# Two units of an output projection moved into the attention stage that comes before it

## The chip, the core and the metric

One core of one Trainium2 chip runs one program, launched once. The metric is device time in microseconds (us). Engines are named as the profile names them: PE (TensorE matmuls; PEld its weight loads), DVE (VectorE), ACT (ScalarE), POOL (GpSimd), SP (SyncE, which here only issues DMAs).

## The reference

One layer of a streaming encoder over 1,024 prompt tokens and 8 streams of 16 new tokens, 1,152 tokens (9 tiles of 128) in all, everything in float32:

```
h = RMSNorm(x)
z = h @ w_in                      # B, C, x_in (gated short convolution), q, k, v (attention)
a = B * causal_dwconv3(C * x_in)  # 1,024 columns
o = differential attention, 8 heads of 128 columns, RMSNorm per head
x = x + concat(a, o) @ w_out      # the output projection, 2048 x 2048
x = x + HierMoE(RMSNorm(x))       # top-1 of 4 expert groups, top-2 of its 8 experts
y = RMSNorm(x)
```

## The kernel before

The kernel is a row of phases, each a block of five instruction streams with waits on semaphores. At the end of a block all engines meet, so no instruction of the next phase starts earlier on any engine. In order: norm and input projection, attention of the streams (`phase_decode`), attention of the prompt (`phase_attend`), output projection with the router's logits (`phase_mix_out`), experts, final norm. The change touches `phase_attend`, `phase_mix_out` and the class `MixWeights`.

**Precision by parts.** Each float32 operand of a large product is kept as two rounded parts, hi and lo, and a product is three matmuls: hi with hi, hi with lo, lo with hi.

**`phase_attend`.** A head has eight row tiles of 128 queries, taken in four pairs of a large and a small one, 32 pairs `n` in all. Each engine's stream is a software pipeline written out by hand over `n` from -2 to 32: scores (PE), maximum (DVE), exponential (ACT), sum ratios (POOL, two tiny instructions per tile), the mix of the two score maps (DVE, L1025, the wait for POOL's ratio before it), transposes (PE, L957), weighted sum with v (PE, L971), the copy of the result (ACT, L1124). POOL also squares the finished heads (L913) and scales them (L918) between ratios, at iterations given in tables. A finished head is turned (four PE transposes per half head) and kept as `o_hi` (ACT, L1135) and `o_lo` (DVE, L1045); heads 0 to 5 and the streams' rows go through this inside the pipeline. Heads 6 and 7 come last: after the pipeline DVE squares, sums and scales head 7 while POOL scales head 6 (L918, the last one), then PE makes the 16 transposes of `LAST_OUTS` (L1003 to L1008) into the four banks of `s_big`. PSUM is full in this phase: `s_big` four banks, `s_small` two, `t_ps` and `o_ps` one each. At the end of its stream SP issues the loads of the first two units of `w_out` (L889), and at the end of its own POOL splits them into hi and lo (L931).

**`phase_mix_out`.** The tokens are taken in two passes (five tiles, then four), the 2,048 output columns in four chunks of 512: eight rounds. A round goes over the 16 row blocks `k` of `w_out`, two at a time: such a pair is a **unit**, 64 units in all, 30 matmuls each in the first pass (2 blocks x 5 tiles x 3). The first four units of a round multiply `o` (heads 0 and 1, then 2 and 3, and so on), the last four multiply `a`. A unit's weights (512 KB) are loaded by SP into one of two `raw` buffers and split by POOL into one of two `hi`/`lo` buffers: a cast (L2186) and a subtraction (L2188). The load of unit i waits for the split of unit i-2; the split of unit i waits until PE has used unit i-2 and, of course, for its load. PE waits for a unit's split before it (L1299 to L1301 are the three matmuls). At the start of the phase ACT issues eight loads of 1,152 KB that bring all of `a` from DRAM (L1351, L1352), and SP issues, in this order, the router's weights `wr` (L1249: 2,048 runs of 144 bytes) and bias `br` (L1250: 128 runs of 144 bytes), the load of unit 2, one chunk of the norm's factors `g`, the load of unit 3, the first tile of `x`, the load of unit 4, and so on.

```
if i >= 2:
    sp.wait_ge(self.split_done, i - 1)
...
for i in range(2, ROUNDS * NQ):
    unit_used(pool, i - 2)
    weights.split(pool, i)
```

Of the kernel before, what the change touches and what calls it, by code (L numbers as in the profile page):

```python
# [29 lines left out]
P = 128  # L30
# [737 lines left out]
    sp.dma_start(v[:, s, :, :], c.io.v_all[0:PROMPT, h * VD:(h + 1) * VD].rearrange("(t p) e -> p t e", p=P)).then_inc(head_loaded[s], 16)  # L768


def phase_attend(c, o_hi, o_lo, q, k_rows, v, head_loaded, first_weights):

    nc, io, sem = c.nc, c.io, c.sem
    QT = PROMPT // P
# [13 lines left out]
    OUTS = ((HEADS, 0), (HEADS, 1), (0, 0), (0, 1), (1, 0), (1, 1), (2, 0), (2, 1), (3, 0), (3, 1), (4, 0), (4, 1), (5, 0), (5, 1))  # L788
    FIRST_OUT = 16
    LAST_OUTS = ((6, 0), (6, 1), (7, 0), (7, 1))  # L790

    def out_at(n):
        return n - FIRST_OUT if 0 <= n - FIRST_OUT < len(OUTS) else None
# [14 lines left out]
    with ExitStack() as mem:  # L808
        def sb(name, shape, dt=F32):
# [24 lines left out]
        squared, summed, guarded, mean_ready = sem("a_squared"), sem("a_summed"), sem("a_guarded"), sem("a_mean_ready")  # L834
        root_ready, rstd_ready, scaled = sem("a_root_ready"), sem("a_rstd_ready"), sem("a_scaled")
        out_turned, out_hi, out_kept = sem("a_out_turned"), sem("a_out_hi"), sem("a_out_kept")
        last_squared, last_turned, last_hi, last_scaled = (sem(f"a_{n}") for n in (
            "last_squared", "last_turned", "last_hi", "last_scaled"))

        s_ps, pr, at = (s_big, s_small), (pr_big, pr_small), (at_big, at_small)  # L840

# [33 lines left out]
            return ps.rearrange("p (a n) -> p a n", a=4) if h == HEADS else ps  # L875

        def last_bank(n):
            return s_big[:, n // 2, (n % 2) * 512:(n % 2 + 1) * 512]

        with nc.Block() as block:  # L880

            @block.sync
            def _(sp):
                sp.dma_start(so[:], io.o_new.rearrange("p (a b) -> p a b", a=HEADS)).then_inc(so_loaded, 16)
                for h in range(2, HEADS):
                    sp.wait_ge(weighed, QT * (h - 1))
                    load_head(c, sp, h, q, k_rows, v, head_loaded)
                for i in range(2):
                    first_weights.load(sp, i)  # L889

            @block.gpsimd
            def _(pool):
                pool.memset(mask_k[:], 1.0).then_inc(mask_step, 1)
                pool.memset(mask_q[:], 0.0).then_inc(mask_step, 1)
                pool.wait_ge(mask_step, 2)
                for m in range(2):
                    pool.memset(mask_q[m * DH:m * DH + 1, 0:P // 2], MASKED).then_inc(mask_step, 1)

                def ratio(kind, n):

                    col = tile(kind, n)
                    pool.wait_ge(inverted[kind], n + 1)
                    pool.tensor_tensor(factor(kind, n), factor(kind, n), l[:, col, 0:1], ALU.mult).then_inc(ratios[kind], 1)
                    pool.wait_ge(ratios[kind], n + 1)
                    pool.tensor_tensor(factor(kind, n), factor(kind, n), c.neglam[:], ALU.mult).then_inc(cf_ready[kind], 1)

                def square_head(h):
                    pool.wait_ge(o_kept, QT * (h + 1))
                    if h > 0:
                        pool.wait_ge(summed, h)  # L910
                    else:
                        pool.wait_ge(so_step, 2)
                    pool.tensor_tensor(square[:], o[:, h], o[:, h], ALU.mult).then_inc(squared, 1)  # L913

                def scale(h):
                    batch = 0 if h == HEADS else [n for n, (h0, h1) in enumerate(BATCHES) if h0 <= h < h1][0]
                    pool.wait_ge(rstd_ready, batch + 1)
                    pool.tensor_tensor(rows_of(h), rows_of(h), per_row(h), ALU.mult).then_inc(scaled, 1)  # L918

                for n in range(-2, PAIRS + 1):  # L920
                    if is_pair(n + 1):
                        ratio(BIG, n + 1)
                    if is_pair(n):
                        ratio(SMALL, n)
                    if n in SQUARES:
                        square_head(SQUARES[n])
                    if n in SCALES:
                        scale(SCALES[n])
                scale(6)
                for i in range(2):  # L930
                    first_weights.split(pool, i)  # L931

            @block.tensor
            def _(pe):
# [48 lines left out]
                for n in range(-2, PAIRS + 1):  # L983
                    if is_pair(n):
                        turn(BIG, n, 0)
                    if out_at(n) is not None:
                        h, half = OUTS[out_at(n)]
                        pe.wait_ge(scaled, SCALED[h])
                        pe.wait_ge(o_kept, 2 * n - 1)
                        turn_out(o_ps[:], h, half).then_inc(out_turned, 1)  # L990
                    if is_pair(n + 2):
                        scores(BIG, n + 2)
                    if is_pair(n):
                        turn(BIG, n, 1)
                    if is_pair(n - 1):
                        weigh(SMALL, n - 1, 0)
                    if is_pair(n + 1):
                        scores(SMALL, n + 1)
                    if is_pair(n):
                        weigh(BIG, n, 0)  # L1000
                        turn(SMALL, n, 0)
                        weigh(BIG, n, 1)
                for n, (h, half) in enumerate(LAST_OUTS):  # L1003
                    if h == HEADS - 1:
                        pe.wait_ge(last_scaled, 1)
                    else:
                        pe.wait_ge(scaled, len(SCALES) + 1)
                    turn_out(last_bank(n), h, half).then_inc(last_turned, 1)  # L1008

            @block.vector  # L1010
            def _(dve):
# [88 lines left out]
                dve.tensor_tensor(rows_of(HEADS - 1), rows_of(HEADS - 1), per_row(HEADS - 1), ALU.mult).then_inc(last_scaled, 1)  # L1100
                for n, (h, half) in enumerate(LAST_OUTS):
                    dve.wait_ge(last_hi, n + 1)
                    out_lo(last_bank(n), h, half)

            @block.scalar
            def _(act):
# [54 lines left out]
                    out_hi_of(last_bank(n), h, half).then_inc(last_hi, 1)  # L1161


def phase_mix_out(c, a_hi, a_lo, o_hi, o_lo, weights):

    nc, io, sem = c.nc, c.io, c.sem
    WC = 4 * P
    NCH = D // WC
    QK = 2
    NQ = KT // QK  # L1170
    AK = 2
    FIRST = (NT + 1) // 2
    PASSES = (tuple(range(FIRST)), tuple(range(FIRST, NT)))
    ROUNDS = 2 * NCH
    with ExitStack() as mem:
        def sb(name, shape, dt=F32):
            return mem.enter_context(nc.sbuf_tensor(name, shape, dt))

        w_hi, w_lo, w_split = weights.hi, weights.lo, weights.split_done
        x = sb("m_x", [P, FIRST, WC])  # L1180
        xg = sb("m_xg", [P, FIRST, WC])
        xgT = sb("m_xgT", [P, 2, 4, P])
# [3 lines left out]
        junk = sb("m_junk", [P, 2, WC])  # L1186
        parts = sb("m_parts", [P, NT, NCH])
        ssq = sb("m_ssq", [P, NT])
        z = mem.enter_context(nc.psum_tensor("m_z", [P, FIRST, WC], F32))
        tp = mem.enter_context(nc.psum_tensor("m_tp", [P, 2, 4, P], F32))  # L1190
        lg_ps = mem.enter_context(nc.psum_tensor("m_lg", [P, 512], F32))
        g_loaded = c.sems("m_g_loaded", 2)
        x_loaded, x1_stored, xg_stored = (c.sems(f"m_{n}", FIRST) for n in ("x_loaded", "x1_stored", "xg_stored"))
        w_used, params = sem("m_w_used"), sem("m_params")
        z_done, x1_ready, xg_ready, squared = sem("m_z_done"), sem("m_x1_ready"), sem("m_xg_ready"), sem("m_squared")
        turned, turned_kept, logits_done = sem("m_turned"), sem("m_turned_kept"), sem("m_logits_done")
        summed, root_done, rstd_done, lg_step = sem("m_summed"), sem("m_root_done"), sem("m_rstd_done"), sem("m_lg_step")
# [35 lines left out]
        with nc.Block() as block:  # L1233

            @block.sync
            def _(sp):
# [9 lines left out]
                        sp.wait_ge(squared, piece(v - 1, s) + 1)  # L1246
                    sp.dma_start(x[:, s, :], rows_of(io.x, v, s)).then_inc(x_loaded[s], 16)

                sp.dma_start(wr[:], io.w_router.rearrange("(k p) n -> p k n", p=P)).then_inc(params, 16)  # L1249
                sp.dma_start(br[:], io.b_router.to_broadcast([P, NR])).then_inc(params, 16)  # L1250
                for v in range(ROUNDS):
                    for q in range(NQ):
                        if v > 0 or q >= 2:
                            weights.load(sp, v * NQ + q)
                        if q == 2:
                            load_g(v)
                        if q >= 3 and q - 3 < len(tiles(v)):
# [1 line left out]

            @block.gpsimd  # L1260
            def _(pool):
                for i in range(2, ROUNDS * NQ):
                    unit_used(pool, i - 2)
                    weights.split(pool, i)

# [1 line left out]
            def _(pe):  # L1267
# [17 lines left out]
                    mm.then_inc(logits_done, 1)  # L1285

                for v in range(ROUNDS):
                    for k in range(KT):
                        i = v * NQ + k // QK
                        if k % QK == 0:  # L1290
                            pe.wait_ge(w_split, i + 1)
# [2 lines left out]
                        for s in slots(v):  # L1294
                            if k == 0 and v > 0:
                                pe.wait_ge(x1_ready, piece(v - 1, s) + 1)
                            hi, lo = cat(k, tiles(v)[s])
                            wh, wl = w_hi[:, i % 2, k % QK, :], w_lo[:, i % 2, k % QK, :]
                            pe.matmul(z[:, s, :], hi, wh, start=(k == 0), stop=False)  # L1299
                            pe.matmul(z[:, s, :], hi, wl, start=False, stop=False)  # L1300
                            mm = pe.matmul(z[:, s, :], lo, wh, start=False, stop=(k == KT - 1))  # L1301
                            if k == KT - 1:
                                mm.then_inc(z_done, 1)
                        if k % QK == QK - 1 and k < KT - 1:
# [857 lines left out]
class MixWeights:  # L2162
# [3 lines left out]
    def __init__(self, c, mem):  # L2166
        nc, shape = c.nc, [P, 2, self.QK, self.WC]
        self.raw = mem.enter_context(nc.sbuf_tensor("m_w_raw", shape, F32))
        self.hi, self.lo = (mem.enter_context(nc.sbuf_tensor(f"m_w_{n}", shape, F32R)) for n in ("hi", "lo"))
        self.loaded, self.hi_done, self.split_done = c.sems("m_w_loaded", 2), c.sem("m_w_hi_done"), c.sem("m_w_split")  # L2170
        self.rows = c.io.w_out.rearrange("(h k p) n -> h p k n", h=2, p=P)

    def load(self, sp, i):
# [7 lines left out]

    def split(self, pool, i):

        s = i % 2
        pool.wait_ge(self.loaded[s], 16 * (i // 2 + 1))
        pool.tensor_copy(self.hi[:, s], self.raw[:, s]).then_inc(self.hi_done, 1)  # L2186
        pool.wait_ge(self.hi_done, i + 1)
        pool.tensor_tensor(self.lo[:, s], self.raw[:, s], self.hi[:, s], ALU.subtract).then_inc(self.split_done, 1)  # L2188


def build(nc, io):
# [7 lines left out]
    with ExitStack() as stack:  # L2199
# [23 lines left out]
        with ExitStack() as mem:  # L2223
# [8 lines left out]
            phase_decode(c, first_keys, keys_loaded, q, k_rows, v, head_loaded)  # L2232
            o_hi, o_lo = cat("o_hi"), cat("o_lo")
            weights = MixWeights(c, mem)
            phase_attend(c, o_hi, o_lo, q, k_rows, v, head_loaded, weights)
            a_hi, a_lo = cat("a_hi"), cat("a_lo")
            phase_mix_out(c, a_hi, a_lo, o_hi, o_lo, weights)
        c.clear_semaphores()
        with ExitStack() as mem:
            c.group_expert = mem.enter_context(nc.sbuf_tensor("group_expert", [1, SLOT_GROUPS], I32))  # L2240
# [56 lines left out]
```

## Time and profile before

| what | value |
|---|---|
| median of 3 runs | 3646.26 us (3644.12 to 3651.1) |
| span of the profiled execution | 3649.7 us |
| PE busy | 3378.6 us, 93% |
| DVE, ACT, POOL busy | 1667.7 us (46%), 1291.5 us (35%), 839.7 us (23%) |
| mean granted TensorE clock | 0.965 of full speed |
| prompt attention | from 1394 us to 1646 us after the span's start |
| output projection | from 1646 us to some 2110 us |

The span runs from the first to the last instruction. The profiled execution has no separate time of its own beside its span; the span lies 1.4 us under the slowest of the three runs and 3.4 us over their median. Times below count from the span's start. A wait is an engine's idle time before an instruction, with what released it.

### The profile page before, as it was taken

Reading aid. Unit: us, or ns where it says so; the run is one execution under the profiler, and the core shown is the slowest. Engines: PE = TensorE matmul, PEld = TensorE weight load, DVE = VectorE, ACT = ScalarE, POOL = GpSimd, SP = SyncE. Lnnn points to the kernel's source line nnn. Section 1 sums busy time; section 2 is a strip of 40 time slices with the busy share of each in tenths; the row PEclk is TensorE's granted clock in tenths of the full one; section 3 lists DMA queues with packets and bytes.
Section 4 is the critical chain, followed back from the end, with each engine's and each line's share of the span. In section 5 each row is a group of like instructions: output and inputs, shape, how many; then the busy total and the mean of one; then the engine's idle time right before and its main releaser. Section 6 shows DMA issues by size and latency. Waiting matters only on the chain. (4 is left out here: it accounts for less than half of the span.)

```text
span 3649.7 us, 51076 instructions
## 1 busy us (share of the span) xinstructions
PE 3378.6 (93%) x18429; PEld 2959.6 (81%) x18430; DVE 1667.7 (46%) x1742; ACT 1291.5 (35%) x1581; POOL 839.7 (23%) x689
## 2 busy tenths in 40 slices
PE   7999999999999887988999959999999999999990
PEld 7999999999999865656888847878888778778770
DVE  5211112100111146871021167558888858856677
ACT  4000000000000034660011037557878757746572
POOL 2223222222222211224445531101111111101010
PEclk9999999999999989998999969999999999999995
DMA  4112111212222292116344459769999969967798
GB/s 153 59 53 66 59 53 53 76 62 74 85 79 66 85 335 75 60 40 225 122 155 143 132 180 361 263 251 343 359 366 357 373 244 371 357 242 251 270 337 355
DMA packets 340683, 692.65 MB, mean 190 GB/s; under 512 B 23034, under 2 KB 150954, under 8 KB 329983
## 3 DMA queue, kind: packets, MB, share of 16 engines
q1 hardware_dynamic: 290340, 586.79, 45.3%
q10 hardware_dynamic: 37163, 66.14, 4.9%
q0 software_dynamic: 13104, 38.69, 3.0%
q8 instruction: 50, 0.82, 0.1%
q14 instruction: 26, 0.21, 0.0%
HBM read 638.29 MB, written 97.28 MB: 202 GB/s over the span
## 5 line engine op out<-in xcount | busy, mean ns | idle before, releaser
L1876 DVE TENSOR_TENSOR e_w_lo<-expert_raw,e_w_hi 128x2048 fp32r<-128x2048 f32 x388 | 872.5, 2287 | 254.7 <-ACT e_w_hi L1788 228.4
L1788 ACT ACTIVATE e_w_hi<-expert_raw 128x2048 fp32r<-128x2048 f32 x388 | 744.5, 1919 | 301.0 <-PE e_gu L1702 252.0
L280 PE MATMUL p_z<-hT_hi,p_w_hi 128*128 128x384 f32 x2256 | 755.0, 335 | 1.6 <-DVE p_xs L399 1.6
L282 PE MATMUL p_z<-hT_hi,p_w_lo 128*128 128x384 f32 x2256 | 753.6, 334 | 0.0
L281 PE MATMUL p_z<-hT_lo,p_w_hi 128*128 128x384 f32 x2256 | 753.6, 334 | 0.0
L280 PEld LDWEIGHTS p_z<-hT_hi,p_w_hi 128*128 128x128 f32 x2256 | 423.5, 188 | 1.9 <-DVE p_xs L399 1.9
L281 PEld LDWEIGHTS p_z<-hT_lo,p_w_hi 128*128 128x128 f32 x2256 | 423.5, 188 | 0.0
L282 PEld LDWEIGHTS p_z<-hT_hi,p_w_lo 128*128 128x128 f32 x2256 | 423.4, 188 | 0.0
L1702 PE MATMUL e_gu<-e_w_hi,e_xT_hi 128*128 128x512 f32 x1216 | 390.1, 392 | 6.3 <-issue 6.2
L1702 PE MATMUL e_gu<-e_w_lo,e_xT_hi 128*128 128x512 f32 x1216 | 387.5, 390 | 0.0
L1702 PE MATMUL e_gu<-e_w_hi,e_xT_lo 128*128 128x512 f32 x1216 | 387.4, 390 | 0.0
L266 POOL CAST p_w_hi<-p_w_raw 128x1024 fp32r<-128x1024 f32 x96 | 100.4, 1046 | 895.2 <-issue 427.4
L1702 PEld LDWEIGHTS e_gu<-e_w_hi,e_xT_hi 128*128 128x128 f32 x1216 | 226.8, 188 | 60.3 <-issue 14.6
L1702 PEld LDWEIGHTS e_gu<-e_w_lo,e_xT_hi 128*128 128x128 f32 x1216 | 228.6, 188 | 48.1
L1702 PEld LDWEIGHTS e_gu<-e_w_hi,e_xT_lo 128*128 128x128 f32 x1216 | 228.6, 188 | 47.8
L736 ACT ACTIVATE d_kT<-d_t 128x512 f32<-128x512 f32 x32 | 19.1, 596 | 662.8 <-PE d_t L619 662.8
L268 POOL TENSOR_TENSOR p_w_lo<-p_w_raw,p_w_hi 128x1024 fp32r<-128x1024 f32 x96 | 235.5, 2453 | 7.7
L486 ACT ACTIVATE p_e_hi<-p_e 128x1152 fp32r<-128x1152 f32 x8 | 9.3, 1168 | 576.0 <-DVEq L438 576.0
L1679 PE MATMUL e_y_ps<-e_w_hi,e_aT_hi 128*128 128x512 f32 x608 | 198.9, 408 | 14.9 <-DVE e_w_lo L1876 6.9
L1542 POOL COPY e_gather_idx<-e_table 128x2 int32 (+1 forms) x33 | 8.2, 248 | 879.6 <-PE e_t L1633 688.8
L1326 DVE TENSOR_TENSOR m_x<-m_z,m_x 128x512 f32<-128x512 f32 x36 | 24.6, 691 | 393.7 <-PE m_z L1301 393.7
L1679 PE MATMUL e_y_ps<-e_w_hi,e_aT_lo 128*128 128x512 f32 x608 | 192.4, 397 | 0.0
(323 smaller groups left out, 4532.3 us busy)
## 6 DMA issues: line engine op xcount, KB each, us to landing
expert_raw<-w_ei SPq DMA_DIRECT2D x256, 1024.0 KB, 8.5
expert_raw<-w_eo SPq DMA_DIRECT2D x128, 1024.0 KB, 10.4
p_w_raw<-w_in SPq DMA_DIRECT2D x96, 512.0 KB, 3.8
m_w_raw<-w_out SPq DMA_DIRECT2D x64, 512.0 KB, 4.1
d_v<-cache_v SPq DMA_DIRECT2D x8, 2048.0 KB, 8.4
rows_back<-expert_rows SPq DMA_DIRECT2D x12, 1024.0 KB, 15.7
n_x<-x SPq DMA_DIRECT2D x9, 1024.0 KB, 5.0
chunks<-p_e ACTq DMA_DIRECT2D x16, 576.0 KB, 2.8
```

What stands on the lines that cost most here:

```text
L266: pool.tensor_copy(w_hi[:, part, :], w_raw[:, part, :]).then_inc(hi_done, 1)
L268: pool.tensor_tensor(w_lo[:, part, :], w_raw[:, part, :], w_hi[:, part, :], ALU.subtract).then_inc(split[half], 1)
L280: pe.matmul(out, w_hi[:, k, :], x_hi[:, xk, cols], start=(k == 0), stop=False)
L281: pe.matmul(out, w_hi[:, k, :], x_lo[:, xk, cols], start=False, stop=False)
L282: mm = pe.matmul(out, w_lo[:, k, :], x_hi[:, xk, cols], start=False, stop=(k == KT - 1))
L486: act.activation(e_hi[:], e[:], ACT.Copy).then_inc(hi_ready, 1)
L736: act.activation(kT[:, b % 2, h, :], t_ps[:, 0, :], ACT.Copy).then_inc(kT_ready[0], 1)
L1326: dve.tensor_tensor(x[:, s, :], z[:, s, :], x[:, s, :], ALU.add).then_inc(x1_ready, 1)
L1679: mm = pe.matmul(y_ps[:, m % 2, :], a_part[:, r, k, :], w_part[:, s, k * 512:(k + 1) * 512], start=(k == 0 and a_part is aT_hi and w_part ...
L1702: return pe.matmul(gu_ps[:, 2 * r + h, :].rearrange("p (b n) -> p b n", b=2), x_part[:, r, k, :], w[:, :, h, :], start=(k == 0 and x_part ...
L1788: act.activation(w_hi[:, s, :], raw[:, r, :], ACT.Copy).then_inc(hi_done, 1)
L1876: dve.tensor_tensor(w_lo[:, s, :], raw[:, r, :], w_hi[:, s, :], ALU.subtract).then_inc(lo_done[r], 1)
```

## The change

- The first two units (0 and 1; heads 0 to 3) are multiplied inside `phase_attend`: unit 0 after the pipeline and before the transposes of the last heads, unit 1 after these. The accumulators `z` (five banks) are laid over `s_big` and half of `s_small`; the 16 last transposes go to the other half of `s_small`, `t_ps`, `o_ps` and, for the fourth, the half of `s_small` again once its first `o_lo` is out.
- POOL's split of these two units is cut into its cast (`round`) and subtraction (`remainder`) and put into the pipeline, at iterations 26 and 28 for unit 0, 30 and 31 for unit 1.
- SP loads units 0 and 1 at the start of `phase_attend`, and units 2 and 3 at its end, into the `raw` buffers that are free by then. Their split stays in `phase_mix_out`.
- In `phase_mix_out` SP issues `wr` and `br` behind the load of unit 7 rather than first, and PE starts at unit 2.

```
@@ phase_attend
+    FIRST_UNITS = 2
+    ROUNDED, LEFT = {26: 0, 30: 1}, {28: 0, 31: 1}
+    UNIT_HEADS = first_weights.QK * FIRST_UNITS
+    OUTS_OF_UNITS = 2 + 2 * UNIT_HEADS
...
         def last_bank(n):
-            return s_big[:, n // 2, (n % 2) * 512:(n % 2 + 1) * 512]
+            return (s_small[:, 1, :], t_ps[:], o_ps[:], s_small[:, 1, :])[n]
...
                 sp.dma_start(so[:], io.o_new.rearrange("p (a b) -> p a b", a=HEADS)).then_inc(so_loaded, 16)
+                for i in range(FIRST_UNITS):
+                    first_weights.load(sp, i)
                 for h in range(2, HEADS):
                     sp.wait_ge(weighed, QT * (h - 1))
                     load_head(c, sp, h, q, k_rows, v, head_loaded)
-                for i in range(2):
+                for i in range(FIRST_UNITS, FIRST_UNITS + 2):
                     first_weights.load(sp, i)
...
                     if n in SCALES:
                         scale(SCALES[n])
+                    if n in ROUNDED:
+                        first_weights.round(pool, ROUNDED[n])
+                    if n in LEFT:
+                        first_weights.remainder(pool, LEFT[n])
                 scale(6)
-                for i in range(2):
-                    first_weights.split(pool, i)
...
+                def first_unit(i):
+                    pe.wait_ge(first_weights.split_done, i + 1)
+                    for k in range(first_weights.QK * i, first_weights.QK * (i + 1)):
+                        for s in range(z.shape[1]):
+                            cols = slice(s * P, (s + 1) * P)
+                            mm = first_weights.products(pe, k, z[:, s, :], o_hi[:, k, cols], o_lo[:, k, cols], k == 0, False)
+                    mm.then_inc(first_weights.used, 1)
+
+                for kind in (BIG, SMALL):
+                    pe.wait_ge(exp_done[kind], 2 * PAIRS)
+                pe.wait_ge(out_kept, OUTS_OF_UNITS)
+                first_unit(0)
                 for n, (h, half) in enumerate(LAST_OUTS):
                     if h == HEADS - 1:
                         pe.wait_ge(last_scaled, 1)
                     else:
                         pe.wait_ge(scaled, len(SCALES) + 1)
+                    if n == 3:
+                        pe.wait_ge(last_lo, 1)
                     turn_out(last_bank(n), h, half).then_inc(last_turned, 1)
+                first_unit(1)
@@ phase_mix_out
+    BEGUN = 2
+    LOADED = 4
...
-                sp.dma_start(wr[:], io.w_router.rearrange("(k p) n -> p k n", p=P)).then_inc(params, 16)
-                sp.dma_start(br[:], io.b_router.to_broadcast([P, NR])).then_inc(params, 16)
                 for v in range(ROUNDS):
                     for q in range(NQ):
-                        if v > 0 or q >= 2:
+                        if v > 0 or q >= LOADED:
                             weights.load(sp, v * NQ + q)
+                        if v == 0 and q == NQ - 1:
+                            sp.dma_start(wr[:], io.w_router.rearrange("(k p) n -> p k n", p=P)).then_inc(params, 16)
+                            sp.dma_start(br[:], io.b_router.to_broadcast([P, NR])).then_inc(params, 16)
...
-                for i in range(2, ROUNDS * NQ):
+                for i in range(BEGUN, ROUNDS * NQ):
                     unit_used(pool, i - 2)
                     weights.split(pool, i)
...
                 for v in range(ROUNDS):
-                    for k in range(KT):
+                    for k in range(QK * BEGUN if v == 0 else 0, KT):
...
@@ MixWeights
     def split(self, pool, i):
+        self.round(pool, i)
+        self.remainder(pool, i)
+
+    def round(self, pool, i):
         s = i % 2
         pool.wait_ge(self.loaded[s], 16 * (i // 2 + 1))
         pool.tensor_copy(self.hi[:, s], self.raw[:, s]).then_inc(self.hi_done, 1)
+
+    def remainder(self, pool, i):
+        s = i % 2
         pool.wait_ge(self.hi_done, i + 1)
         pool.tensor_tensor(self.lo[:, s], self.raw[:, s], self.hi[:, s], ALU.subtract).then_inc(self.split_done, 1)
```

## Rows read from the trace of the kernel before

**Rows 1.** Waits from 1625 to 1730 us: in total us, times, longest.

```profile
POOL m_w_hi L2186 <- DMA m_w_raw<-w_out: 27.3, 2, 24.4
...
PE m_z L1299 <- POOL m_w_lo L2188: 11.3, 1, 11.3
```

**Rows 2.** Timeline of PE, end of attention to unit 4: start, us, instruction, [idle before].

```profile
1628.93 1.06 PE L957 MATMUL a_t<-ident,a_pr_small 128*128 128x128 f32 x4
...
1630.88 1.13 PE L971 MATMUL a_o_ps<-a_v,a_at_small 128*128 128x128 f32 x8 [0.46 <-DVE a_at_small L1032]
1638.79 3.67 PE L977 MATMUL a_s_big<-ident,a_o 128*128 128x128 f32 x16 [6.78 <-POOL a_o L918]
1645.90 0.76 PE L1299 MATMUL m_z<-m_w_hi,o_hi 128*128 128x512 f32 x1 [3.44 <-PEq L880]
...
1673.43 0.79 PE L1299 MATMUL m_z<-m_w_hi,o_hi 128*128 128x512 f32 x1 [11.31 <-POOL m_w_lo L2188]
...
1682.63 0.39 PE L1299 MATMUL m_z<-m_w_hi,o_hi 128*128 128x512 f32 x1
...
1689.43 0.39 PE L1299 MATMUL m_z<-m_w_hi,a_hi 128*128 128x512 f32 x1
```

**Rows 3.** DMA queues in 1654 to 1656 us: packets, MB, share of 16 engines.

```profile
q10 hardware_dynamic: 175, 0.76, 96.3%
q1 hardware_dynamic: 175, 0.03, 7.7%
```

**Rows 4.** The same in 1664 to 1666 us.

```profile
q10 hardware_dynamic: 132, 0.58, 70.6%
q1 hardware_dynamic: 128, 0.25, 31.8%
```

**Rows 5.** DMA issues: units 3 and 4 of the weights; last figure is us to landing.

```profile
m_w_raw<-w_out SPq DMA_DIRECT2D x1, 512.0 KB, 23.2
...
m_w_raw<-w_out SPq DMA_DIRECT2D x1, 512.0 KB, 6.4
```

**Rows 6.** Timeline of POOL.

```profile
1577.64 1.90 POOL L918 TENSOR_TENSOR a_o<-a_o,a_rstd 128x1024 f32<-128x1024 f32 x1
...
1607.99 0.19 POOL L905 TENSOR_TENSOR a_cf<-a_cf,neglam 128x1 f32<-128x1 f32 x1
...
1621.46 0.19 POOL L905 TENSOR_TENSOR a_cf<-a_cf,neglam 128x1 f32<-128x1 f32 x1
...
1626.59 0.19 POOL L905 TENSOR_TENSOR a_cf<-a_cf,neglam 128x1 f32<-128x1 f32 x1
1635.80 2.93 POOL L918 TENSOR_TENSOR a_o<-a_o,a_rstd 128x1024 f32<-128x1024 f32 x1 [9.02 <-DVE a_rstd L1052]
...
1643.21 2.34 POOL L2188 TENSOR_TENSOR m_w_lo<-m_w_raw,m_w_hi 128x1024 fp32r<-128x1024 f32 x1
1669.92 1.04 POOL L2186 CAST m_w_hi<-m_w_raw 128x1024 fp32r<-128x1024 f32 x1 [24.36 <-DMA m_w_raw<-w_out]
1671.03 2.34 POOL L2188 TENSOR_TENSOR m_w_lo<-m_w_raw,m_w_hi 128x1024 fp32r<-128x1024 f32 x1
```

**Rows 7.** Timeline of DVE: two mixes of small tiles of one width, the last mix, the last `o_lo`.

```profile
1578.78 0.90 DVE L1025 SCALAR_TENSOR_TENSOR a_pr_small<-a_pr_small,a_cf 128x128 f32<-128x128 f32 x1
...
1609.28 0.34 DVE L1025 SCALAR_TENSOR_TENSOR a_pr_small<-a_pr_small,a_cf 128x128 f32<-128x128 f32 x1
...
1626.81 0.75 DVE L1025 SCALAR_TENSOR_TENSOR a_pr_small<-a_pr_small,a_cf 128x512 f32<-128x512 f32 x1 [0.57 <-POOL a_cf L905]
...
1640.66 3.31 DVE L1045 SCALAR_TENSOR_TENSOR o_lo<-a_s_big,a_hn_col,o_hi 128x512 fp32r<-128x512 f32 x4 [3.68 <-ACT o_hi L1135]
```

**Rows 8.** Timeline of ACT: the first `o_hi` of the last heads.

```profile
1639.94 0.69 ACT L1135 ACTIVATE o_hi<-a_s_big,a_hn_col 128x512 fp32r<-128x512 f32 x1 [4.50 <-PE a_s_big L977]
```

**Rows 9.** Windows of 2 us: length, busy us (count) of PE, PEld, DVE, ACT, POOL, granted clock, DMA.

```profile
1632.00:1634.00 2.00, 0.01 (x1) 0.00 (x0) 1.61 (x2) 1.76 (x3) 0.00 (x0) 0.96 0.00 0
...
1664.00:1666.00 2.00, 0.00 (x0) 0.00 (x0) 0.00 (x0) 0.00 (x0) 0.00 (x0) 0.64 1.02 414
```

More of the change, by code:

```diff
@@ L768, in load_head, with phase_attend @@
     sp.dma_start(v[:, s, :, :], c.io.v_all[0:PROMPT, h * VD:(h + 1) * VD].rearrange("(t p) e -> p t e", p=P)).then_inc(head_loaded[s], 16)
-def phase_attend(c, o_hi, o_lo, q, k_rows, v, head_loaded, first_weights):
+def phase_attend(c, o_hi, o_lo, q, k_rows, v, head_loaded, first_weights, z):
     nc, io, sem = c.nc, c.io, c.sem
@@ L836, in phase_attend @@
         out_turned, out_hi, out_kept = sem("a_out_turned"), sem("a_out_hi"), sem("a_out_kept")
-        last_squared, last_turned, last_hi, last_scaled = (sem(f"a_{n}") for n in (
-            "last_squared", "last_turned", "last_hi", "last_scaled"))
+        last_squared, last_turned, last_hi, last_lo, last_scaled = (sem(f"a_{n}") for n in (
+            "last_squared", "last_turned", "last_hi", "last_lo", "last_scaled"))
         s_ps, pr, at = (s_big, s_small), (pr_big, pr_small), (at_big, at_small)
@@ L1102, in _ @@
                     dve.wait_ge(last_hi, n + 1)
-                    out_lo(last_bank(n), h, half)
+                    out_lo(last_bank(n), h, half).then_inc(last_lo, 1)
             @block.scalar
@@ L1161, in _, with phase_mix_out @@
                     out_hi_of(last_bank(n), h, half).then_inc(last_hi, 1)
-def phase_mix_out(c, a_hi, a_lo, o_hi, o_lo, weights):
+def phase_mix_out(c, a_hi, a_lo, o_hi, o_lo, weights, z):
     nc, io, sem = c.nc, c.io, c.sem
@@ L1177, in sb @@
             return mem.enter_context(nc.sbuf_tensor(name, shape, dt))
-        w_hi, w_lo, w_split = weights.hi, weights.lo, weights.split_done
+        w_split, w_used = weights.split_done, weights.used
         x = sb("m_x", [P, FIRST, WC])
@@ L1188, in phase_mix_out @@
         ssq = sb("m_ssq", [P, NT])
-        z = mem.enter_context(nc.psum_tensor("m_z", [P, FIRST, WC], F32))
+        mem.enter_context(nc.psum_tensor("m_z_place", [P, FIRST, WC], F32))
         tp = mem.enter_context(nc.psum_tensor("m_tp", [P, 2, 4, P], F32))
@@ L1193, in phase_mix_out @@
         x_loaded, x1_stored, xg_stored = (c.sems(f"m_{n}", FIRST) for n in ("x_loaded", "x1_stored", "xg_stored"))
-        w_used, params = sem("m_w_used"), sem("m_params")
+        params = sem("m_params")
         z_done, x1_ready, xg_ready, squared = sem("m_z_done"), sem("m_x1_ready"), sem("m_xg_ready"), sem("m_squared")
@@ L1297, in _ @@
                             hi, lo = cat(k, tiles(v)[s])
[L1298 to L1301, printed above, removed]
+                            mm = weights.products(pe, v * KT + k, z[:, s, :], hi, lo, k == 0, k == KT - 1)
                             if k == KT - 1:
@@ L2170, in __init__ @@
         self.loaded, self.hi_done, self.split_done = c.sems("m_w_loaded", 2), c.sem("m_w_hi_done"), c.sem("m_w_split")
+        self.used = c.sem("m_w_used")
         self.rows = c.io.w_out.rearrange("(h k p) n -> h p k n", h=2, p=P)
@@ L2186, in split, with products @@
         pool.tensor_copy(self.hi[:, s], self.raw[:, s]).then_inc(self.hi_done, 1)
+    def remainder(self, pool, i):
+        s = i % 2
         pool.wait_ge(self.hi_done, i + 1)
         pool.tensor_tensor(self.lo[:, s], self.raw[:, s], self.hi[:, s], ALU.subtract).then_inc(self.split_done, 1)
+    def products(self, pe, i, out, hi, lo, first, last):
+        wh, wl = self.hi[:, i // self.QK % 2, i % self.QK, :], self.lo[:, i // self.QK % 2, i % self.QK, :]
+        pe.matmul(out, hi, wh, start=first, stop=False)
+        pe.matmul(out, hi, wl, start=False, stop=False)
+        return pe.matmul(out, lo, wh, start=False, stop=last)
 def build(nc, io):
@@ L2234, in build @@
             weights = MixWeights(c, mem)
-            phase_attend(c, o_hi, o_lo, q, k_rows, v, head_loaded, weights)
+            with ExitStack() as later:
+                z = later.enter_context(nc.psum_tensor("m_z", [P, (NT + 1) // 2, weights.WC], F32))
+            phase_attend(c, o_hi, o_lo, q, k_rows, v, head_loaded, weights, z)
             a_hi, a_lo = cat("a_hi"), cat("a_lo")
-            phase_mix_out(c, a_hi, a_lo, o_hi, o_lo, weights)
+            phase_mix_out(c, a_hi, a_lo, o_hi, o_lo, weights, z)
         c.clear_semaphores()
```

## The prediction, written before the changed kernel was built

> **What bounds the kernel now.** I read the page first (PE busy in 93% of the span, so time is won where PE stands still), then the waits around the change, then the engines' timelines there. The waits from 1625 to 1730 us name one large stop of PE, 11.3 us for POOL's split of unit 2, and behind it POOL's own wait for that unit's load, 24.4 us [rows 1]. PE's timeline gives the whole stretch [rows 2]. The last product of the attention ends at 1630.88 + 1.13 = 1632.01, unit 4 starts at 1689.43: 57.4 us. In order they hold:
> - 6.78 idle until POOL has scaled head 6;
> - 3.67 for the 16 transposes;
> - 3.44 idle, until POOL has split units 0 and 1 and the block has closed;
> - units 0 and 1, from 1645.90 to 1673.43 - 11.31 = 1662.12: 16.2;
> - 11.31 idle for unit 2;
> - unit 2, 9.20 (1673.43 to 1682.63);
> - unit 3, 6.80 (1682.63 to 1689.43).
>
> Unit 3 is a unit at full speed, 30 matmuls at 0.227 us. Unit 2 took 2.4 more because its first matmuls came out of the long stop at half the clock: in the window from 1664 the granted clock is 0.64, so it fell to 1.2 GHz after the stop began [rows 9].
>
> Why the load was late stands in the DMA queues. From 1654 to 1656 queue q10 (the loads of `a`) and q1 (SP's) each moved 175 packets, 0.76 MB and 0.03 MB [rows 3]: packets alternate one to one, and the 144-byte packets of `wr` and `br` were paired with packets of 4.6 KB. 2,048 + 128 small packets at 175 per 2 us are 25 us, nearly the whole of the transfer of `a`, and units 2 and 3 were queued behind them: unit 3 took 23.2 us to land, unit 4, later and without `wr` ahead, 6.4 [rows 5].
>
> **The change, part by part.** I rebuild the 57.4 us.
>
> *Splits inside the pipeline.* Three of the four POOL pieces fall on a DVE mix. A mix of 128 columns took 0.90 us while POOL's scale ran to 1577.64 + 1.90 = 1579.54, and 0.34 without it; it ended 0.14 after POOL [rows 6, 7]. So a mix waits for POOL's large instruction and ends some 0.2 less than its own length after it. The cast of unit 0 (iteration 26) meets only maxima that read PSUM, which I take as free: nothing. Its subtraction (28) can start at about 1608.1, behind the ratio of 1607.99, and runs 2.34 to 1610.5; the mix of 1609.28 then ends at 1610.65, not 1609.62. Its transposes come at 1610.55 anyway, so of the 1.0 only 0.2 reaches PE. The cast of unit 1 (30), from about 1621.6 for 1.04, would hold the mix behind the ratio of 1621.46 by up to 0.8; PE would feel 0.4. The subtraction (31) starts with the ratio of 1626.59 done, at about the moment of the last mix, 1626.81. If POOL is first it runs to 1629.1 and the mix ends at 1629.65, not 1627.56; the transposes, at 1628.93 before [rows 2], start some 0.7 later. Sum: 1.3 us. If DVE always wins it is nothing; if all three pieces lie on the path in full it is 1.04 + 2 x 2.34 = 5.7. I take 1.3, built from the case that the rows show. The Trainium skill's page "SBUF — State Buffer", section "Who interferes with whom", has the rule: a DVE instruction with two SBUF inputs and a GpSimd instruction that reads SBUF lock each other out for the whole instruction. The rows agree for POOL's two-input form (0.90 against 0.34); no row shows its cast against a mix. By the rule in full the sum would be 0.2 to 0.6 longer, since the 0.2 of overlap would go.
>
> *Unit 0.* It needs `z` free (all exponentials done, which they are) and starts at once: 6.8 us in place of idle time. Before, the clock was still full (0.96 in the window 1632 to 1634) when PE stopped [rows 9]; now PE goes on. I take full speed; at the worst it costs 9.2 as unit 2 did. It ends at 1632.0 + 1.3 + 6.8 = 1640.1. POOL's scale of head 6 ended at 1635.80 + 2.93 = 1638.73 [rows 6]; 1.3 later that is 1640.0, so the transposes wait for nothing.
>
> *Transposes.* The first three sets of four take some 0.53 each at full clock (half of 3.67 / 4 = 0.92, plus a little). The fourth waits for the first `o_lo`. Before, from the start of the first set to `o_hi` took 1639.94 - 1638.79 = 1.15, of which some 0.4 was the slower clock, and `o_lo` starts 0.72 after that and takes 3.31 / 4 = 0.83 [rows 2, 7, 8]: 2.3 us after the first transpose, plus 0.6 for the last set. I take 3.0; bounds 2.2 (no wait) and 4.5 (half clock).
>
> *Unit 1.* 6.8 us, now the last thing of the block; ACT and DVE finish their last halves beside it. Then the block closes: before, 1643.21 + 2.34 = 1645.55 to 1645.90, 0.35 [rows 2, 6], and about 0.15 for the tail of the last matmul.
>
> *Unit 2.* Its load was issued in the attention (the `raw` buffer is free at 1610.5; unit 3's at 1629.1), so its data lie there. But its split is still in the new block and starts when this opens: 1669.92 to 1671.03 + 2.34, 3.5 us [rows 6]. This stands bare on the path, 4 us of idle PE in all. I take the clock to fall again and unit 2 to cost 9.2; if it does not, 6.8. Unit 3's split (3.5) is covered by unit 2; unit 3 costs 6.8.
>
> *Sum.* 1.3 + 6.8 + 3.0 + 6.8 + 0.15 + 0.35 + 3.5 + 9.2 + 6.8 = 37.9 us in place of 57.4: **19.5 us less**, unit 4 at about 1669.9.
>
> *What has to arrive by then.* Unit 4's load is issued when unit 2 is split, 1653.9, behind `g` and one tile of `x` (128 packets each). In step with q10 at 2 KB a packet, q1 moves 128 packets in 2 us [rows 4]: its 256 packets take 4 us, and 6.4 was measured in just this company [rows 5]. It lands at 1660.3; POOL is free to split it when unit 2 is used, 1663.2, and PE stalls only if it lands after 1666.4. Cover 6 us. Units 5 to 7 follow at 6.8 us each with the same margin or more. The first quarter of `a` is 512 packets, 8 us at that rate, done by 1660, needed at 1669.9.
>
> *`wr` and `br`, moved.* They are now issued behind unit 7's load, at about 1675, ahead of the fifth tile of `x` and of unit 8's load. `a` (2,048 packets, 26 us at 132 per 2 us plus the small start) is then nearly through, so the 2,176 packets no longer go one for one with large ones. The floor is 0; at the paired rate 25 us, they would end at 1700, with unit 8's load behind them, when its split should start at 1691.5. I take 0: the cover is gone only if `a` is still moving.
>
> *SP's queue in the attention.* Two loads of 512 KB at its start stand ahead of head 2's, which waits for the first head anyway: 0. Units 2 and 3 wait at the end of SP's stream with nothing behind them: 0.
>
> Everything after unit 4 is unchanged, PE goes from matmul to matmul there, and each later phase begins where all engines meet, so I carry the 19.5 to the end. The span is 3649.7, giving 3630.2; the median of the runs shown is 3.4 lower, so against it the forecast is 3646.3 - 19.5 = 3626.8 us.
>
> **Rivals.**
> - *The late load only moves on to unit 4.* `a` still floods the queues from the block's start. If unit 4 needs 23.2 us as unit 3 did [rows 5], it lands at 1677.1, is split at 1680.6, and runs 2.4 longer after the stop: 13.1 lost, 6.4 left, 3639.9 us. For it: the same 9.4 MB. Against it: the small packets ahead of it are gone. 0.07; no change by the bound below.
> - *POOL's pieces cost the attention more.* All in full (5.7), and unit 0 and the transposes at half clock (2.4 and 1.5): 8.3 lost, 3635.1 us. 0.08; still faster.
> - *Slower: the clock.* PE's work is now cut by short waits (the last mix, the fourth transposes, the bare split). If the clock stayed at 1.2 GHz over all this and did not come back, each matmul costs 0.227 more (the 2.4 counted for unit 2 are 11 such). It decides from 19.5 / 0.227 = 86 matmuls beyond these. Over units 0 to 7 that would be 229 x 0.227 = 52.0 us, 32.5 slower than before: 3678.8 us. For it: the clock fell in the stop before unit 2 [rows 9]. Against it: unit 2 is back at full speed within its 30. 0.02.
> - *The change does not do what it says*: another engine holds PE before unit 0 (a wait for ACT or DVE), and unit 0 fills no idle time. Then 6.8 are lost, 3633.6 us, 0.03.
>
> **Numbers.** The forecast has 0.80. A measurement of this kernel can tell about 0.2%, 7.3 us, from no change. Faster: 0.80 + 0.08 + 0.03 = 0.91; same 0.07; slower 0.02. The range: at the low end no loss in the attention (1.3) and unit 2 at full clock (2.4) give 3623.1, and the runs scatter by some 4: 3619. At the high end the second and fourth rivals and 2 of scatter: 3637.
>
> **What would show it.** Right: PE at work from about 1633 to 1650 with a gap under 1 us; one wait of about 4 us for POOL's split at the block change; unit 4 near 1670; unit 2's load landed long before; no wait on unit 8. Wrong: a wait of PE for POOL before unit 4 or 8, a last mix on DVE of over 3 us, or half clock in units 0 and 1.

## The result and the profile after

The changed kernel takes 3626.14 us (median of 4 runs, 3624.13 to 3628.1), the kernel before 3645.54 (median of 4): ratio 0.9944, 95% interval 0.9933 to 0.9956, 19.4 us less. The forecast was 3626.8.

The two profiled spans differ by more, 3649.7 against 3623.2 us. 5.9 of it lie before the attention of the prompt starts: its first PE instruction comes at 1394.21 us before and at 1388.29 after, behind stages that the change does not touch. So times are compared from that instruction on. The **stretch** from it to unit 4's first matmul is 295.2 us before and 277.0 after, 18.2 less.

PE's timeline (start, us, instruction, [idle before]), which answers to [rows 2]:

```profile
1623.52 1.12 PE L965 MATMUL a_t<-ident,a_pr_small 128*128 128x128 f32 x4 [1.54 <-DVE a_pr_small L1049]
...
1625.52 2.05 PE L979 MATMUL a_o_ps<-a_v,a_at_small 128*128 128x128 f32 x8 [0.46 <-DVE a_at_small L1056]
...
1627.22 0.77 PE L2227 MATMUL m_z<-m_w_hi,o_hi 128*128 128x512 f32 x1
...
1635.60 0.60 PE L985 MATMUL a_s_small<-ident,a_o 128*128 128x128 f32 x4
...
1637.85 0.63 PE L985 MATMUL a_s_small<-ident,a_o 128*128 128x128 f32 x4 [0.78 <-DVE o_lo L1069]
1638.23 0.48 PE L2227 MATMUL m_z<-m_w_hi,o_hi 128*128 128x512 f32 x1
...
1649.18 0.79 PE L2227 MATMUL m_z<-m_w_hi,o_hi 128*128 128x512 f32 x1 [3.87 <-POOL m_w_lo L2222]
...
1665.27 0.39 PE L2227 MATMUL m_z<-m_w_hi,a_hi 128*128 128x512 f32 x1
```

Unit 0 follows the last product at once, the transposes wait only for the fourth bank (0.78), unit 1 closes the block, and the 11.31 us stop of [rows 2] is gone. What is left is one stop of 3.87 us, for POOL's split of unit 2. POOL's and DVE's timelines show the pieces of the splits and the mixes beside them, as in [rows 6, 7]:

```profile
1615.03 1.04 POOL L2216 CAST m_w_hi<-m_w_raw 128x1024 fp32r<-128x1024 f32 x1
...
1620.57 2.35 POOL L2222 TENSOR_TENSOR m_w_lo<-m_w_raw,m_w_hi 128x1024 fp32r<-128x1024 f32 x1
...
1645.67 1.04 POOL L2216 CAST m_w_hi<-m_w_raw 128x1024 fp32r<-128x1024 f32 x1 [11.38 <-POOLq L884]
...
1659.84 1.04 POOL L2216 CAST m_w_hi<-m_w_raw 128x1024 fp32r<-128x1024 f32 x1 [7.29 <-DMA m_w_raw<-w_out]
1660.96 2.40 POOL L2222 TENSOR_TENSOR m_w_lo<-m_w_raw,m_w_hi 128x1024 fp32r<-128x1024 f32 x1
```

```profile
1615.13 1.35 DVE L1049 SCALAR_TENSOR_TENSOR a_pr_small<-a_pr_small,a_cf 128x384 f32<-128x384 f32 x1 [0.57 <-POOL a_cf L911]
...
1620.65 2.81 DVE L1049 SCALAR_TENSOR_TENSOR a_pr_small<-a_pr_small,a_cf 128x512 f32<-128x512 f32 x1 [0.57 <-POOL a_cf L911]
```

The last mix took 2.81 us in place of 0.75 [rows 7], and ended 0.54 behind POOL. The mix beside unit 0's subtraction took 1.36 in place of 0.34. The Trainium skill's page "SBUF — State Buffer", section "Who interferes with whom", says of the ports that DVE and POOL share that whoever issues first has them for the whole instruction and the other fully blocks; the order agrees, but the mix ended sooner behind POOL than its own 0.75. The 1.35 beside the cast shows that POOL's one-input form holds the mix too, which no row of before could show.

The granted clock in windows of 2 us (columns as in [rows 9]) fell to half before unit 0, was full again within this unit, and fell once more at the bare split:

```profile
1626.00:1628.00 2.00, 2.00 (x10) 1.90 (x9) 0.09 (x1) 0.38 (x2) 0.00 (x0) 0.50 0.03 12
...
1632.00:1634.00 2.00, 2.00 (x10) 1.65 (x9) 0.54 (x1) 0.00 (x0) 2.00 (x1) 1.00 0.03 8
...
1650.00:1652.00 2.00, 2.00 (x6) 1.52 (x6) 0.00 (x0) 0.00 (x0) 1.92 (x2) 0.50 1.03 404
```

### The profile page after: what moved, and what is told of

It reads as the page before. It is cut to its first block and busy times, and to the rows that moved or that the text cites. A ratio compares the mean times of both kernels' runs of the same rounds, so it can differ in the third digit from the quotient of the medians.

```text
span 3623.2 us, 51079 instructions
## 1 busy us (share of the span) xinstructions
PE 3369.6 (93%) x18429; PEld 2949.8 (81%) x18430; DVE 1671.1 (46%) x1742; ACT 1291.2 (36%) x1581; POOL 838.9 (23%) x689
## 5 line engine op out<-in xcount | busy, mean ns | idle before, releaser
L268 POOL TENSOR_TENSOR p_w_lo<-p_w_raw,p_w_hi 128x1024 fp32r<-128x1024 f32 x96 | 235.5, 2453 | 7.7
L1703 PE MATMUL e_y_ps<-e_w_lo,e_aT_hi 128*128 128x512 f32 x608 | 192.0, 397 | 0.0
```

Source lines behind the costliest of these rows:

```text
L268: pool.tensor_tensor(w_lo[:, part, :], w_raw[:, part, :], w_hi[:, part, :], ALU.subtract).then_inc(split[half], 1)
L1703: mm = pe.matmul(y_ps[:, m % 2, :], a_part[:, r, k, :], w_part[:, s, k * 512:(k + 1) * 512], start=(k == 0 and a_part is aT_hi and w_part ...
```

## The experiments

Beside the stretch, the end of the first round is given: the first DVE addition of `m_x`, counted from the same instruction, 320.0 us before and 301.7 after. A profile is one execution.

**1. The router's weights first again** (the changed kernel with one part undone).

```
+                sp.dma_start(wr[:], ...)
+                sp.dma_start(br[:], ...)
                 for v in range(ROUNDS):
...
-                        if v == 0 and q == NQ - 1:
-                            sp.dma_start(wr[:], ...)
-                            sp.dma_start(br[:], ...)
```

> The changed kernel, with the router's weights and bias (wr, br) issued first in the output projection again. Measured in the trace from the attention's first PE instruction to the first matmul of unit 4: 295.2 us before, 277.0 after. Theory (their 2,176 small packets alternate one to one with the packets of a, and every later load on SP's queue stands behind them): 25 us of small packets from the block's start, then g, a tile of x and unit 4's load, so unit 4 lands some 30 us into the block, PE stops 13 to 16 us in front of unit 4 and runs 2.4 us more at half clock behind the stop: stretch 292 to 295, time 3641 to 3645 us. Rival (loading units 2 and 3 early is what removed the stop; unit 4 has 19 us of cover in units 2 and 3): no stop over 3 us, time 3625 to 3630 us.

Measured: 3641.72 us against 3646.82, ratio 0.9983 (0.9973 to 0.9993); stretch 291.4, end of the round 318.8. Of PE's timeline:

```profile
1683.78 0.80 PE L2226 MATMUL m_z<-m_w_hi,a_hi 128*128 128x512 f32 x1 [10.55 <-POOL m_w_lo L2221]
```

A stop like that of 11.31 us is back, only two units later. Unit 4's load was issued at 1657.54 and POOL had it at 1680.27. The stop was 2.5 us under the least that was expected, since the small packets did not take 25 us: `wr` landed 16.5 and `br` 17.8 us after its issue. But the rival is out: as long as the small packets go first, moving the units and loading two early gains 5.1 us by the medians, 3.8 up to unit 4 and 1.2 by the end of the round.

**2. The router's weights moved, alone** (the kernel before with the lines of experiment 1 where the change has them).

> The kernel before, with wr and br issued behind the load of unit 7 in the first round, and nothing else changed: all units stay in the output projection. Theory (the stop of PE before unit 2 comes from the small packets alone): unit 2's load, now first in SP's queue, lands within 7 us of its issue and is split while PE still works on unit 1; the 11.3 us stop and the 2.4 us of half clock in unit 2 go: 13.7 us less, stretch about 281.5, time about 3632 us. Rival (the 9.4 MB of a hold the load back): unit 2 lands after 20 us as before, at most 3 us gained, time over 3642 us.

Measured: 3632.85 us, ratio 0.9965 (0.9952 to 0.9977), 14.0 us less; stretch 281.7, end of the round 306.4, 13.5 less. POOL's wait before unit 2's cast is now one for PE's unit 0, not for the load:

```profile
1650.01 1.04 POOL L2187 CAST m_w_hi<-m_w_raw 128x1024 fp32r<-128x1024 f32 x1 [9.85 <-PE m_z L1302]
```

As the theory said, to 0.2 us. Moving two DMA issues gives more than two thirds of the whole change. Here the small packets go out when `a` is nearly through, and `wr` landed 6.5 us after its issue, in place of 16.9 in the kernel before. The first line is `wr` in the kernel before, the second is SP's queue here from 1678 to 1680, when no packet of `a` moved any more:

```profile
m_wr<-w_router SPq DMA_DIRECT2D x1, 288.0 KB, 16.9
...
q1 hardware_dynamic: 1512, 0.26, 82.2%
```

So 1,512 packets, nearly all of them small, pass in 2 us alone and 175 beside the full `a` [rows 3]: it is `a` that slows the small packets, and they that hold back what stands behind them.

**3. Units 2 and 3 loaded late** (`LOADED = 2`, the second pair of loads at the end of SP's attention stream left out).

> The changed kernel, with the loads of units 2 and 3 issued at the start of the output projection and not at the end of the attention. Theory (the split of unit 2 stands bare on PE's path, so its load does too when it is late): the load takes 5 to 6 us from issue to landing beside a's loads, and PE's wait before unit 2 grows from 3.9 to 9 to 10 us: stretch 282 to 283, time 3631 to 3632 us. Rival (the early load is covered anyway, since the block's start costs as much): stretch 277 to 278, no change.

Measured: 3635.41 us, ratio 0.9968 (0.9956 to 0.9981); stretch 282.5. PE's wait before unit 2:

```profile
1657.80 0.80 PE L2225 MATMUL m_z<-m_w_hi,o_hi 128*128 128x512 f32 x1 [9.86 <-POOL m_w_lo L2220]
```

So the early load is worth 6 us of that stop. The median is 3.4 us above what was expected, the stretch and the wait are as expected.

**4. The pieces of unit 1's split behind the mixes**

```
+                    if n >= 30:
+                        pool.wait_ge(mixed[SMALL], min(n + 1, PAIRS))
                     if n in ROUNDED:
```

> The changed kernel, with POOL's cast of unit 1 (iteration 30) and its subtraction (31) held back until DVE has done the mix of the same iteration. Theory (POOL's large instructions lock DVE's two-input mix out): the last mix goes from 2.81 back to 0.75 us, the one before it from 1.35 to 0.62, and unit 0 starts 1.5 to 2 us earlier, counted from the attention's first PE instruction; stretch 275 to 275.5, time 3624 to 3625 us, which the timing alone cannot tell. Rival (the late end is the half clock of PE at that place and not the mix): the mixes become short but unit 0 starts less than 0.5 us earlier.

Measured: 3624.94 us, ratio 0.9945 (0.9928 to 0.9961); stretch 271.4. The mixes are short again:

```profile
1617.62 0.62 DVE L1051 SCALAR_TENSOR_TENSOR a_pr_small<-a_pr_small,a_cf 128x384 f32<-128x384 f32 x1 [0.57 <-POOL a_cf L911]
...
1622.76 0.75 DVE L1051 SCALAR_TENSOR_TENSOR a_pr_small<-a_pr_small,a_cf 128x512 f32<-128x512 f32 x1 [0.58 <-POOL a_cf L911]
```

From the mix of iteration 27 to unit 0 are 31.8 us in the changed kernel and 28.4 here, 3.4 less rather than 1.5 to 2: 2.4 up to the end of the last mix, and 0.9 behind it, where the clock stayed full up to unit 0, so that the last products took 1.16 and not 2.05 us. Unit 0 itself, at full clock, took 7.0 and not 8.4, and so the stretch came out 3.6 us under the least that was expected.

**5. Only the last piece held back** (the same with `n >= 31`).

> The changed kernel, with only POOL's subtraction of unit 1 (iteration 31) held back behind the last mix. Theory (it is this piece that delays the end, and the cast of iteration 30 only by 0.4 us): last mix 0.75 us, the one before it 1.35; unit 0 1 to 3 us earlier than in a profile of the changed kernel with the same clock at that place; if the granted clock stays at full speed over the end of the attention here too, the long wait of PE for the last mix is what lets it fall. Rival (the clock's fall there has nothing to do with that wait): half clock in the last 10 us as in the kernel before.

One run, 3627.24 us: last mix 0.75, the one before it 1.35, 28.7 us from iteration 27 to unit 0, clock full. So 3.0 of the 3.4 us are this one piece, and 0.3 are the cast. That PE's long wait for the last mix is what lets the clock fall is not shown by this: in the kernel before it fell without such a wait (last section).

**6. The changed kernel once more.**

> The changed kernel once more, as it is, beside the two below and for a second profile of the end of the attention. Stretch from the attention's first PE instruction to unit 4: 277 us in the first profile. Theory (the granted clock of the last 15 us of the attention differs by execution): unit 0 starts 238 to 243 us after that instruction, as in the three profiles with the same attention so far (238.9, 242.6, 240.0), and a piece of half clock lies before it. Rival (it is a fixed cost): 238.9 within 0.3. Time 3624 to 3629 us.

Measured: 3631.41 us (3623.7 to 3634.84) against 3645.67, ratio 0.995 (0.9933 to 0.9968). Unit 0 began at 242.7 us, but from iteration 27 on it is the same 31.8: the difference, up to 4 us, arises earlier in the attention, whose instructions are the same. So neither side is quite right: the end is a fixed cost, the beginning differs by execution.

**7. Unit 2's split inside the attention**

```
                 scale(6)
+                pool.wait_ge(first_weights.used, 1)
+                first_weights.split(pool, FIRST_UNITS)
...
-                for i in range(BEGUN, ROUNDS * NQ):
+                for i in range(BEGUN + 1, ROUNDS * NQ):
```

> The changed kernel, with POOL's split of unit 2 moved from the output projection to the end of its stream in the attention, behind a wait for unit 0's last matmul; POOL has nothing else to do there for 11 us. Theory (the 3.9 us of PE idle before unit 2 are this split and nothing else, and the clock falls because of them): PE goes from unit 1 to unit 2 with less than 1 us between, unit 2 takes 6.8 to 7.0 and not 9.3 us: 3.4 + 2.4 = 5.8 us less, from unit 0's start to unit 4's 32.3 us rather than 38.05; time 3619 to 3621 us. Rival (the block's change costs as much by itself): a gap over 3 us remains and the clock falls all the same.

Measured: 3627.97 us, ratio 0.9952 (0.9936 to 0.9967), not separable from the changed kernel beside it (3631.41). PE's timeline and POOL's:

```profile
1645.21 0.47 PE L2229 MATMUL m_z<-m_w_hi,o_hi 128*128 128x512 f32 x1 [0.32 <-PEq L884]
...
1662.80 0.50 PE L2229 MATMUL m_z<-m_w_hi,a_hi 128*128 128x512 f32 x1 [3.72 <-POOL m_w_lo L2224]
```

```profile
1659.29 1.04 POOL L2218 CAST m_w_hi<-m_w_raw 128x1024 fp32r<-128x1024 f32 x1 [10.53 <-DMA m_w_raw<-w_out]
```

The stop before unit 2 shrank to 0.32 and unit 2 took 6.9 us: the split was all of it. But a new stop of 3.72 stands before unit 4, whose load is late. From unit 0 to unit 4 it is 36.0 and not 32.3 us; that stop was missing in the expectation.

**8. Experiments 4 and 7 together, twice.**

> Both edits: POOL's pieces held back behind the mixes of iterations 30 and 31, and unit 2's split inside the attention. Theory: the two do not touch each other and their gains add: unit 0 at 235.6 to 237.5 us after the attention's first PE instruction, unit 4 some 32 us later, stretch 267.5 to 270, time 3617 to 3620 us. Rival (the split of unit 2 is hidden already when the attention ends sooner, or collides with DVE's last work): no more than split2_inside alone.

> The kernel with both edits once more, beside the one above on the same chip: 3620 to 3624 us, stop of 3.7 us before unit 4 in its profile, stretch 270 to 274 us.

Measured: 3621.93 us against 3645.67, ratio 0.994 (0.9925 to 0.9955), and 3627.05 against 3645.78, 0.9946 (0.9933 to 0.996); stretch 270.2 and 271.6, with the stop before unit 4 (3.65, 3.72). Both times are above what was expected. Unit 0 came about as forecast, at 235.5 and 236.9 us, but unit 4 34.7 us later and not 32. The end of the round is at 297.9 and 299.4 us, no less than in experiments 4 and 5 without unit 2's split inside (296.1, 297.9); and experiment 7 reached that end at 302.3, the changed kernel at 301.7. So without unit 4's load, moving this split gave nothing that shows at the end of the round.

**9. And unit 4's load in the attention** (`LOADED = 5`, one more load at the end of SP's stream there).

> The kernel with both edits, and unit 4's load issued at the end of the attention as well (its raw buffer is free once unit 2 is split there, and no other transfer runs). Theory (the 3.7 us stop before unit 4 in split2_inside and both is unit 4's load, which shares the queues with a and stands behind g and a tile of x): the stop goes, from unit 0's start to unit 4's 30.8 to 31.2 us in place of 34.7, stretch 266 to 267 us, and unit 4 keeps the clock (6.8 rather than 9 us); time 4 to 6 us under both, about 3616 us. Rival (it is a's own first quarter that unit 4 waits for, or the load only gives its place to the next one): a stop of 2 us or more remains before unit 4 or appears before unit 5, and under 3 us are gained.

Measured: 3621.49 us against 3645.78, ratio 0.9938 (0.9924 to 0.9951); stretch 266.4, end of the round 294.6, the shortest of all. Unit 4 follows unit 3 without a stop, from unit 0 in 30.8 us. PE's remaining waits:

```profile
1664.32 0.47 PE L2231 MATMUL m_z<-m_w_hi,a_hi 128*128 128x512 f32 x1 [1.76 <-DMA a_lo<-conv_lo]
1672.53 0.47 PE L2231 MATMUL m_z<-m_w_hi,a_hi 128*128 128x512 f32 x1 [1.15 <-DMA a_lo<-conv_lo]
```

Part of the rival holds: `a` itself, not its weights, now stops units 5 and 6 by 2.9 us. This kernel is the best tried: 25.4 us under before in its profiled first round (320.0 to 294.6), 24.3 by the medians. Its intervals overlap with those of the changed kernel, so that it is faster than that is read from the profile, not from the times.

## Why the prediction was right, step by step

- *The stop and its cause.* Right, and shown: experiment 2 removes it by moving `wr` and `br` alone, experiment 1 brings it back by undoing that alone. The Trainium skill's page "DMA: Bandwidth & Descriptors", section "Queues, rings and completion order", has the rule that a DMA engine goes round between its queues packet by packet; [rows 3] agree in their counts, 175 to 175.
- *The small packets, 25 us.* Too long: `wr` landed 16.9 us after its issue and `br` 19.3. From 1646 to 1650, while `a` was setting in, SP's queue moved 738 packets in the first 2 us and 321 in the next, and only from then on some 175.
- *What the prediction did not say:* that the two parts do not add. Moved units alone gained 1.2 us by the end of the first round, the router's weights alone 13.5, both 18.2. It named the mechanism but gave the credit for the stop to the rebuilt path as a whole.
- *Splits inside the pipeline, 1.3 us.* Measured 1.97, from the mix of iteration 27 to the last product's end before (1602.21 to 1632.01, 29.8) and to unit 0's start after (1595.45 to 1627.22, 31.8). The distances between the small mixes give 0.2 for unit 0's subtraction (6.64 to 6.85), 0.4 for unit 1's cast (5.13 to 5.52), both as forecast. The last piece was mis-sized: 0.7 forecast, 1.4 by what is left. The mix ended as worked out and the transposes started 0.75 later behind it, as forecast; but PE then ran its last products at half clock (2.05 in place of 1.13), which cost the other 0.6.
- *Unit 0, 6.8 us at full clock.* Wrong: 8.38 (1627.22 to 1635.60); its first matmuls ran at half clock. The bound of 9.2 held. Half clock in unit 0 was one of the forecast's own signs of being wrong.
- *Transposes, 3.0:* 2.63. *Unit 1 and the block's end, 7.3:* 1638.23 to 1645.31, then 3.87 of waiting in which the 3.5 of the split lie: together 10.95, forecast 10.8. *Unit 2, 9.2:* 9.29, the clock had fallen. *Unit 3:* 6.80.
- *Sum.* 1.97 + 8.38 + 2.63 + 10.95 + 9.29 + 6.80 = 40.0 us in place of 37.9, so 17.4 gained from the attention's end to unit 4 and not 19.5. The 0.8 up to the 18.2 of the stretch came earlier in the attention. That the measured 3626.14 lies 0.7 us from the forecast is therefore luck in part: the path was mis-sized by 2.1, the profiled spans differ by 5.9 more before the attention and 2.3 more behind the stretch, and the medians gave 19.4 here and 14.3 in experiment 6.
- *Unit 4's load, cover 6 us.* Wrong, without effect on the time: issued at 1649.15, it landed after 10.6 and not 6.4 us, and its split ended at 1663.36, 1.9 us before PE wanted it. The 6.4 us of [rows 5] were not measured in the same company: `a` ended during that load (q10 moved 130 packets from 1674 to 1676, 39 in the next 2 us, then none). Experiment 7 used the cover up and stopped there.
- *`wr` and `br` moved, 0 us.* Right in the time, with less cover than thought. 2,048 packets at 132 in 2 us are 31 us, not 26, and `a` ran until some 1682 us; `wr` landed 12.4 us after its issue. Unit 8's load stood behind it, and its split ended at 1691.20, 1.3 us before PE wanted it.
- *The rivals.* The late load did not reach PE; the attention lost 2.0 us and not 5.7; the clock fell twice and came back each time; nothing held PE before unit 0.

## What to carry to other kernels

When a transfer is late, look at what stands ahead of it in its own queue and count packets, not bytes: beside the loads of `a`, 306 KB in 144-byte pieces took 17 to 19 us to land, the loads queued behind them 20.6 to 23.2, and two lines of reordering gave most of what the larger change gave. Work moved into an idle stretch pays only if the next wait does not move along with it; after each removed stop, ask which load is now the last to arrive (units 2, 4 and then `a` itself). A large POOL instruction put behind the short one that releases DVE started before DVE did, both times here (1615.03 against 1615.13, 1620.57 against 1620.65); one more wait, so that DVE goes first, was worth 3 us up to unit 0.

## What the runs showed of the hardware

The granted clock at the attention's end was not expected. In all seven profiles without the last piece held back, it fell to half in the last 10 us of the attention's pipeline. In the five of these that have the last piece there, the last products and the start of unit 0 ran at half clock. The other two, the kernel before and experiment 2, have no pieces; there it fell earlier, at the product of the last big tile (2.04 and 2.05 us in place of 1.13), and was full again for the last products (1.13). In all five with the piece held back (experiments 4, 5, 8 twice, 9) it stayed full into unit 0. PE's long wait for the last mix (1.54 us) cannot be all of it: in the 5 us before the fall in the kernel before, PE had waited 0.84 us at the most, as in experiment 4, where the clock stayed full. PE's work up to that point is nearly the same in both sets, so what tips it is open.
